# Query and key projections by seven block products, and some work at other places in the order

## The reference

```python
h = rmsnorm(x, norm_w)                    # (512, 1024)
proj = h @ w_in                           # split into:
#   dsa_qkv: 3 groups x (q, k, v) x 8 heads x 64;  dsa_z: 512
#   gdn_qkv: 3 x 512;  gdn_z: 512;  gdn_b, gdn_a: 8 each;  gate_a, gate_b: 1024 each
q, k = rope(q), rope(k)                   # t * cos + rotate_half(t) * sin, half = 32 of 64
o_a = dilated_mixture(q, k, v)            # windowed attention of 3 dilations, joined by softmax of their lse
y_a = (o_a * silu(dsa_z)) @ w_up_a
cqkv = silu(causal_depthwise_conv(gdn_qkv))
o_b = rmsnorm(gated_delta_rule(l2norm(q), l2norm(k), v, g(gdn_a), sigmoid(gdn_b)))
y_b = (o_b * silu(gdn_z)) @ w_up_b
x = x + (sigmoid(gate_a) * y_a + sigmoid(gate_b) * y_b) @ w_out
x = rmsnorm(x, final_norm_w)
```

## Time and profile before

| | us |
|---|---|
| median of 3 runs | 2187.51 |
| lowest, highest | 2183.54, 2192.11 |
| profiled execution | 2183.56 |
| its span | 2181.9 |
| mean granted PE clock | 0.964 |

### The profile page before, as it was taken

How to read it: one execution, slowest core, us unless ns; L and a number is a source line. 1 busy time by engine, 2 the same in 40 slices (tenths; PEclk the granted TensorE clock), 3 DMA queues, 4 the chain that set the end, 5 groups by cost and what they waited for, 6 DMA issues and landing times. The chain is left out here.

```text
span 2181.9 us, 31075 instructions
## 1 busy us (share of the span) xinstructions
PE 2028.5 (93%) x12920; PEld 1299.0 (60%) x12920; DVE 952.8 (44%) x1958; ACT 509.0 (23%) x1038; POOL 205.0 (9%) x202
## 2 busy tenths in 40 slices
PE   8999989989999899999998998897998999999987
PEld 3445767756567566685694464683885555544543
DVE  6672055633452425458414677738644221111102
ACT  1000163142122112353023255325222111100011
POOL 0001102302320233000000001301200000000001
PEclk9999999999899999999999999899799999999999
DMA  4222200110011773111122010000007999999996
GB/s 174 76 75 74 84 20 30 60 53 30 25 36 35 293 310 126 48 59 49 39 72 96 25 34 30 2 15 16 3 20 310 406 424 427 424 426 424 427 425 269
DMA packets 51692, 325.73 MB, mean 149 GB/s; under 512 B 6368, under 2 KB 9056, under 8 KB 33248
## 3 DMA queue, kind: packets, MB, share of 16 engines
q1 hardware_dynamic: 50256, 319.01, 36.9%
q0 software_dynamic: 1152, 4.19, 0.5%
q10 hardware_dynamic: 144, 0.52, 0.1%
HBM read 311.65 MB, written 9.96 MB: 147 GB/s over the span
## 5 line engine op out<-in xcount | busy, mean ns | idle before, releaser
L3700 PE MATMUL psum<-m_ring,m_xg 128*64 128x512 f32 x1024 | 226.2, 597 | 21.5 <-issue 20.4
L3700 PEld LDWEIGHTS psum<-m_ring,m_xg 128*64 128x64 f32 x1024 | 77.1, 138 | 167.3 <-issue 166.0
L419 PE MATMUL psum<-h,wring 128*128 128x512 f32 (+1 forms) x416 | 166.7, 549 | 10.8 <-PEq L93 5.6
L723 PE MATMUL psum<-x,wring 128*128 128x512 f32 x384 | 167.7, 599 | 6.8 <-DMA wring<-in_w1f 6.8
L723 PEld LDWEIGHTS psum<-x,wring 128*128 128x128 f32 x384 | 73.8, 193 | 99.7 <-issue 91.2
L3685 PEld LDWEIGHTS psum<-m_sel,m_htok 128*128 128x128 f32 x1024 | 118.3, 194 | 13.7 <-issue 12.2
L419 PEld LDWEIGHTS psum<-h,wring 128*128 128x128 f32 x416 | 78.4, 195 | 77.3 <-issue 65.5
L3685 PE MATMUL psum<-m_sel,m_htok 128*128 128x128 f32 x1024 | 122.6, 279 | 1.4 <-DVE m_sel L3676 1.4
L3710 DVE TENSOR_TENSOR m_hid<-rstd,psum 64x512 f32<-64x512 f32 x32 | 22.1, 691 | 232.1 <-ACT rstd L3706 221.7
L3725 PE MATMUL psum<-m_ring,m_hid_t 128*64 128x512 f32 x512 | 113.4, 595 | 1.0 <-issue 1.0
L3706 ACT ACTIVATE rstd<-psum 64x512 f32<-64x512 f32 x32 | 18.8, 588 | 324.7 <-PE psum L3700 313.4
(11 more groups left out here) (687 smaller groups left out, 3507.4 us busy)
## 6 DMA issues: line engine op xcount, KB each, us to landing
m_ring<-in_w_gate SPq DMA_DIRECT2D x32, 2048.0 KB, 26.9
m_ring<-in_w_up SPq DMA_DIRECT2D x32, 2048.0 KB, 28.3
m_ring<-in_w_down SPq DMA_DIRECT2D x64, 1024.0 KB, 24.6
wring<-in_w1f SPq DMA_DIRECT2D x60, 512.0 KB, 3.4
ada_ring<-in_w_ada SPq DMA_DIRECT2D x12, 2048.0 KB, 12.4
wring<-in_w2f SPq DMA_DIRECT2D x31, 512.0 KB, 3.4
expert_rows<-tmp SPq DMA_DIRECT2D x14, 512.0 KB, 28.9
wring<-in_w1v SPq DMA_DIRECT2D x12, 512.0 KB, 3.4
```

The source lines that it names most:

```text
L419: return nc.tensor.matmul(place(t, out), lhs, rhs, start=(k == 0), stop=(k == KD - 1))
L723: m = nc.tensor.matmul(K.psum[:, banks[t % 4]], ws.weights(first + t, k), h[:, k], start=(k == 0), stop=(k == KD - 1))
L3700: m = nc.tensor.matmul(K.psum[i * SLOTS:(i + 1) * SLOTS, UP + s], W.xg[:, k, s], w[:, k], start=(k == 0), stop=(k == KD - 1))
```

## The change

- `roped` uses `Pairs`: 12 pairs of which the first is plain. POOL makes the four differences of the weighted x (into v's not yet used part) and four folds per pair. ACT copies the parts into `raws` (gatedB, free at that time) and copies each whole tile once more with its 32-row quarters exchanged into `tmp` (four activations, `swap`). VectorE adds the parts, multiplies raw with cos into the output, `tmp` with sin, and adds. The sine table has its sign exchanged, as the rows are now exchanged first.
- `first_norm` gives the eight multiplications for h positions 0.12 to 0.47, so that they stand between the pairs.
- The SiLU of z moves from the end of `values` to `dilated_join`, behind its Exp; the join's last product waits for it (`zed`).
- `gdn_inputs` loses its sync program; its two loads are the first of `conv`'s sync program, under a global semaphore `ba_landed`. The two programs of the other side are laid out over 36 instead of 45.
- `out_project`: the first half of the next-to-last `total` goes ahead of the last part; ACT's squares get other positions.

```diff
@@ -548,6 +548,7 @@
...
         for k in range(KD):
+            yield 0.12 + 0.05 * k
             nc.vector.tensor_tensor(h[:, k], x[:, k], rate, ALU.mult).then_inc(K.normed, 1)
@@ -706,43 +707,77 @@
...
...
-def roped(nc, K, h, out, cos, sin, banks):
-
-    n, quarter, ws = 24, HD // 2, K.stream
-    first = ws.take(n)
+def roped(nc, K, h, out, cos, sin, diffs, folds, raws, banks):
+
+    n, quarter, ws = 12, HD // 2, K.stream
+    first = ws.take(2 * n)
+    two = Pairs(nc, K, lambda q: first + 2 * q, lambda q: (h, diffs), folds, banks, plain=1, ready=K.weighted)
+    raw = lambda q: lambda i: raws[:, 2 * (q % 2) + i]
+
+    def gpsimd(eng, sem):
+        yield 0.0
+        eng.wait_ge(K.weighted, KD)
+        two.halve(eng, nc.gpsimd, sem, h, diffs)
+        for q in range(n):
+            yield q / n
+            two.fold(eng, nc.gpsimd, sem, q)
...
     def tensor(eng, sem):
-        for t in range(n):
-            yield t / n
-            eng.wait_ge(*ws.arrived(first + t))
-            if t >= 4:
-                eng.wait_ge(sem["emptied"], t - 3)
-            for k in range(KD):
-                if t == 0:
-                    eng.wait_ge(K.weighted, k + 1)
-                m = nc.tensor.matmul(K.psum[:, banks[t % 4]], ws.weights(first + t, k), h[:, k], start=(k == 0), stop=(k == KD - 1))
-            m.then_inc(ws.used, 1)
+        for q in range(n):
+            for at in two.multiply(eng, sem, q, (1, 3, 2, 4)):
+                yield (q + at) / n
+
+    def scalar(eng, sem):
+        def swap(t):
+            two.whole(eng, sem, t // 2, t % 2)
+            if t >= 2:
+                eng.wait_ge(sem["roped"], t - 1)
+            of = raw(t // 2)(t % 2)
+            for p0 in range(0, P, quarter):
+                to = p0 ^ quarter
+                m = nc.scalar.activation(K.tmp[to:to + quarter, t % 2], of[p0:p0 + quarter], ACT.Copy)
+            m.then_inc(sem["swapped"], 1)
+
+        for q in range(n):
+            for i in range(4):
+                yield (q + (0.2, 0.36, 0.5, 1.05)[i]) / n
+                if q >= 2 and i < 2:
+                    eng.wait_ge(sem["roped"], 2 * (q - 2) + i + 1)
+                if q < two.plain and i == 2:
+                    swap(2 * q)
+                if q >= two.plain and i == 3:
+                    swap(2 * q)
+                two.copy(eng, sem, q, i, raw(q))
+                if q and i == 0:
+                    swap(2 * q - 1)
+        swap(2 * n - 1)
...
     def vector(eng, sem):
-        for t in range(n):
-            yield (t + 1.1) / n
+        def turn(t):
             if t == 0:
                 eng.wait_ge(K.tables, 2)
-            eng.wait_ge(ws.used, first + t + 1)
-            if t >= 2:
-                eng.wait_ge(sem["roped"], t - 1)
-            ps = K.psum[:, banks[t % 4]]
-            for p0 in range(0, P, quarter):
-                to, of = p0 ^ quarter, slice(p0, p0 + quarter)
-                nc.vector.tensor_tensor(K.tmp[to:to + quarter, t % 2], ps[of], sin[of], ALU.mult)
-            to, scaled, turned = out[:, t], K.tmp[:, t % 2], (ps, cos)
+            two.whole(eng, sem, t // 2, t % 2)
+            of, scaled, to, by = raw(t // 2)(t % 2), K.tmp[:, t % 2], out[:, t], cos
             if t >= 8:
-                to, scaled, turned = to.rearrange("p (a i) -> p a i", a=TT), strided(scaled), (strided(ps), strided(cos))
-            nc.vector.tensor_tensor(to, turned[0], turned[1], ALU.mult).then_inc(sem["emptied"], 1)
-            eng.wait_ge(sem["emptied"], t + 1)
+                of, scaled, to, by = strided(of), strided(scaled), to.rearrange("p (a i) -> p a i", a=TT), strided(cos)
+            nc.vector.tensor_tensor(to, of, by, ALU.mult).then_inc(sem["turned"], 1)
+            eng.wait_ge(sem["swapped"], t + 1)
+            nc.vector.tensor_tensor(K.tmp[:, t % 2], K.tmp[:, t % 2], sin, ALU.mult).then_inc(sem["turned"], 1)
+            eng.wait_ge(sem["turned"], 2 * t + 2)
             nc.vector.tensor_tensor(to, to, scaled, ALU.add).then_inc(sem["roped"], 1)
...
-    return Program(["emptied", "roped"], sync=ws.requests(first, n), tensor=tensor, vector=vector)
+        for q in range(n):
+            yield (q + 0.3) / n
+            if q:
+                turn(2 * q - 1)
+            for i in range(3):
+                yield (q + (0.6, 0.75, 0.9)[i]) / n
+                two.add(eng, sem, q, i, raw(q))
+            yield (q + 0.95) / n
+            turn(2 * q)
+        turn(2 * n - 1)
+
+    return Program(["swapped", "turned", "roped"] + two.SEMS, sync=ws.requests(first, 2 * n), gpsimd=gpsimd, tensor=tensor, scalar=scalar, vector=vector)
@@ -806,10 +841,6 @@
...
                 two.copy(eng, sem, q, i, raw(q))
-        for q in range(nz // 2):
-            for i in range(2):
-                two.whole(eng, sem, q, i)
-                nc.scalar.activation(z[:, 2 * q + i], z[:, 2 * q + i], ACT.Silu)
@@ -1153,6 +1184,8 @@
...
         nc.scalar.activation(low, low, ACT.Exp).then_inc(sem["exped"], 1)
+        for m in range(4):
+            nc.scalar.activation(z[:, m], z[:, m], ACT.Silu).then_inc(sem["zed"], 1)
@@ -1182,9 +1215,10 @@
...
             link(nc.vector.tensor_tensor(gated[:, m], gated[:, m], tmp, ALU.add))
+            eng.wait_ge(sem["zed"], m + 1)
             nc.vector.tensor_tensor(gated[:, m], gated[:, m], z[:, m], ALU.mult)
...
-    return Program(["ordered", "diffed", "exped", "weighed", "spread", "joined", "v"], tensor=tensor, scalar=scalar, vector=vector)
+    return Program(["zed", "ordered", "diffed", "exped", "weighed", "spread", "joined", "v"], tensor=tensor, scalar=scalar, vector=vector)
@@ -1214,7 +1248,7 @@
...
                                        [(K.halves, a["levelc"]), (K.gdn_gain[:], a["gdn_gain"]), (window, a["mask0"]), (causal, a["mask1"]), (order[:], a["order"])], 7),
-                  follow((168, roped(nc, K, x1, qk, cos, sin, range(4))), (113, values(nc, K, h, v, z, range(4, 8), diffs, folds))))
+                  follow((168, roped(nc, K, x1, qk, cos, sin, v[:].rearrange("p g u n -> p (g u n)")[:, 4 * CTX * KD // 2 // 2:].rearrange("p (i k n) -> p i k n", i=4, n=CTX), folds, gatedB, range(4))), (113, values(nc, K, h, v, z, range(4, 8), diffs, folds))))
         with ExitStack() as ph2:
@@ -1468,8 +1502,8 @@
...
     def vector(eng, sem):
-        def total(t):
-            for i in range(2):
+        def total(t, which=(0, 1)):
+            for i in which:
                 eng.wait_ge(sem["squared"], 2 * t + i + 1)
@@ -1508,13 +1542,15 @@
...
             more(q, 2)
+            if q == n - 1:
+                total(KD - 2, (0,))
             yield (q + 1.01) / n
             part(q, 3)
-        total(KD - 2)
+        total(KD - 2, (1,))
...
         for t in range(KD):
-            yield (t + 1.3) / KD
+            yield (t // 2 + (0.65 + 0.5 * (t % 2) if t < 2 else 0.93 + 0.13 * (t % 2))) / n
             two.whole(eng, sem, t // 2, t % 2)
@@ -2195,19 +2231,13 @@
...
...
-def gdn_inputs(nc, K, a, h, ba, beta, w_ba, bank, rep):
-
-    def sync(eng, sem):
-        yield 0.0
-        eng.dma_start(w_ba[:], a["w1ba"]).then_inc(sem["loaded"], 16)
-        eng.dma_start(rep[:], a["rep"]).then_inc(sem["rep"], 16)
-        eng.wait_ge(sem["rep"], 16)
+def gdn_inputs(nc, K, h, ba, beta, w_ba, bank):
...
             if t == 0:
-                eng.wait_ge(sem["loaded"], 16)
+                eng.wait_ge(K.ba_landed, 32)
             for k in range(KD):
@@ -2218,7 +2248,7 @@
...
...
-    return Program(["loaded", "rep", "done"], sync=sync, tensor=tensor, scalar=scalar)
+    return Program(["done"], tensor=tensor, scalar=scalar)
@@ -2243,7 +2273,7 @@
...
         x_c, folds = sb("g_xc", [P, 4, S + 3], p2), sb("g_folds", [P, 4, KD // 2 * P], p2)
-        weave(nc, "gp", conv(nc, K, h, diffs, folds, x_c, qkv, range(4)), in_turn((27, join), (12, gdn_inputs(nc, K, a, h, ba, beta, w_ba, 4, seeds.rep)), over=45))
+        weave(nc, "gp", conv(nc, K, h, diffs, folds, x_c, qkv, range(4), [(w_ba[:], a["w1ba"]), (seeds.rep[:], a["rep"])]), in_turn((27, join), (12, gdn_inputs(nc, K, h, ba, beta, w_ba, 4)), over=36))
     held.close()
@@ -2274,7 +2304,7 @@
...
...
-def conv(nc, K, h, diffs, folds, x_c, qkv, banks):
+def conv(nc, K, h, diffs, folds, x_c, qkv, banks, loads):
@@ -2326,7 +2356,15 @@
...
...
-    return Program(["convd", "v"] + two.SEMS, sync=ws.requests(first, 2 * n), gpsimd=gpsimd, tensor=tensor, scalar=scalar, vector=vector)
+    def sync(eng, sem):
+        yield 0.0
+        for to, of in loads:
+            eng.dma_start(to, of).then_inc(K.ba_landed, 16)
+        for at in ws.requests(first, 2 * n)(eng, sem):
+            yield at
+        eng.wait_ge(K.ba_landed, 16 * len(loads))
+
+    return Program(["convd", "v"] + two.SEMS, sync=sync, gpsimd=gpsimd, tensor=tensor, scalar=scalar, vector=vector)
@@ -4088,8 +4126,8 @@
...
                       24 + len(values) + 4 + 12 + 4 + len(merges[0]) + len(merges[1]) + len(outs))
```

(6 more changed lines are left out.)

## The result

The changed kernel takes 2160.86 us (median of 4 runs, 2160.04 to 2164.92), the kernel before in the same comparison 2185.53 (2178.57 to 2192.11): ratio 0.9892, interval 0.9872 to 0.9912, or 24.7 us. Forecast were 2160.9 and 26.6 us. The profiled execution took 2161.64, its span 2159.9.

The account below looks back on a forecast made before the run. PE, busy 93% of the span, was taken as the bound. 17.5 - 1.5 - 1.6 + 3.5 + 2.0 + 5.5 + 0.5 + 0.7 = 26.6 us off the median 2187.51 gave 2160.9 us; range 2153 to 2168, with rivals and run spread 2149 to 2174.

Parts of the forecast that it names:

- Seven products, 17.5 less 1.5 less 1.6: Query and key projections: less PE work saves 17.5 us, minus 1.5 for VectorE-POOL collisions and 1.6 waiting at pair 1.
- charge of 1.5 for collisions: Projections: 0.3 us lost in each of six pairs with both strides and h, rounded to 1.5 us (0 to 12).
- the start of pair 1: Projections: PE waits for POOL's first folds after the plain pair, costing 1.6 us (0.5 to 5).
- rival B: Projections: VectorE and POOL obstruct each other and set the pace, about 1 us more in ten pairs; 2171 us, chance 0.12.
- it just holds: Projections, strided pairs with h: VectorE is free at 8.9 us, its adds end near 10, PE needs them at 10.4.
- rival C: Projections: ACT's swap copies, a us each, pace PE; at a = 1.2, 34 us lost, 2195 us; chance 0.04.
- It decides from about a = 1.1: Projections: the time per ACT swap copy, a in us, from which late copies were said to decide; 0.61 was expected.
- h between the pairs, 0: Projections: h is needed only 120 us later, so moving its normalisation costs 0, apart from 0.69 us VectorE work per pair.
- SiLU, 3.5 and 2.0: End of first stage: moving z's SiLU saves 3.5 us of PE wait, and 2.0 (0 to 3) of low clock in dilated attention.
- Beta loads and layout, 5.5 and 0.5: Convolution stage: early beta weights save 5.5 us of wait and low clock; the join over 36 saves 0.5 (-1 to 1.5).
- Output sums, 0.7: End of output projection: last squares start about 0.6 us earlier and context norm is not blocked; 0.7 us saved (0 to 1.5).
- squares no longer block the context norm: Output projection: reordered squares stop holding up the context norm, counted within the 0.7 us saving.

Follow-up runs that it names:

- second trace: The changed kernel run once more, unchanged, in five rounds against the kernel before (also traced again): 2159.32 us (6 runs), ratio 0.9884.
- first experiment: The kernel before with only the seven-product projections, the exchanged sine sign and h normalised between the pairs: 2166.7 us, ratio 0.992.
- the kernel with the earlier differences: The changed kernel with the four differences of weighted x made by VectorE, not POOL, and beta groups later: 2155.72 us; 2153.72 when repeated.

## Why the prediction was right, step by step

- **Seven products, 17.5 less 1.5 less 1.6.** The pace was as read from the earlier trace rows: 12.09 us per pair, forecast 12.1. The charge of 1.5 for collisions was not needed, no pair from 2 to 11 waits; the start of pair 1 cost 2.32 instead of 1.6. The first and fourth fold ended at 26.30 and 31.33, hardly later than in the sum (near 26 and 31), but PE came to them at 25.18 and not at 25.8. In the second trace it cost 1.54, of which 0.98 were a wait for VectorE's adds; the prediction looked for no such wait at pair 1. In sum 15.8 and 14.6 us (two traces, each against its own before), forecast 14.4.
- **Collisions, rival B.** The estimate that it just holds was right. In the changed kernel's pair from 98.83 VectorE is busy for 9.46 of 12.09 us, where its operations alone are 7.7. With the product for h it is free 8.7 us after the pair's start (in the sum 8.9), the first two adds end at 9.4, and PE needs them at 10.4. Two added operations per tile turned it into B and worse. Collisions go the way of the rule of the Trainium skill ("SBUF — State Buffer", "Who interferes with whom"): a VectorE product with two SBUF inputs that took 0.69 us alone took 2.84 us beside a POOL difference of 2.78, and it ended 0.55 us after that difference. These are the rows of the changed kernel:

```profile
21.85 2.78 POOL L226 TENSOR_TENSOR v<-x,v 128x1024 f32<-128x1024 f32 x1
22.34 2.84 DVE L548 TENSOR_TENSOR rstd<-rstd,gatedA 128x512 f32<-128x512 f32 x1
```

- **Swap copies, rival C.** 0.628 us for 32x512, forecast 0.61; with a = 0.91 its sum gave 0.8 us per pair where 0.67 of wait and 0.93 of pair length were seen. "It decides from about a = 1.1" hides that by the same sum copy 2 is late from a = 0.81 on.
- **h between the pairs, 0.** "Cost 0" is true of the changed kernel, so the sum is right. What the prediction missed is what the move is worth: it did not ask what the old place would have cost beside the new work. It is 9.8 us, more than half of the projections' gain. The fault was to price the move in the old schedule, where VectorE's late start hurt nobody, and not in the new one, where the adds of pair 1 free PE's banks.
- **SiLU, 3.5 and 2.0.** 3.34, and 2.1 or 0.7 (by the trace of before that one takes). The wait was there in every trace, the clock's fall varies.
- **Beta loads and layout, 5.5 and 0.5.** 4.74 and 3.08: this is the term that was most oversized. The wait goes from 2.08 to 0.33, and one of two waits for VectorE's adds goes (0.92 and 0.94 before, 0.93 after). From the start of the wait to the third group of products behind the first beta group PE took 10.72 and 10.83 us before and takes 7.36 and 7.54 now: 3.3 us, not 5.5. The term's 3.4 us of clock was priced as if it went with the wait, and it doesn't always. The first experiment, with the whole wait but no fall, took 7.37. In two traces with the changed order (the experiments with the SiLU and with the output sums back) the clock did not fall there, and the stage took 104.9; so it did with the later beta groups. The second trace's 1.8 us more come from the stage's start: there 64 small matmuls run at the low clock in both traces, without a wait that the change touches, and for longer in the second (the first trace's row, then the second's):

```profile
330.71 7.63 PE L1167 MATMUL psum<-d_stat,order 32*128 32x8 f32 x64
...
331.35 9.15 PE L1167 MATMUL psum<-d_stat,order 32*128 32x8 f32 x64
```

- **Output sums, 0.7.** 2.97. Undersized: I did not follow the context squares in ACT's queue, though "squares no longer block the context norm" was the right mechanism.
- The hit to a tenth of a us is luck. The forecast started from 2187.51 for the kernel before, which is 2185.53 beside the changed one, and its gain was 1.9 us too large against the timed one; the two errors cancel. Against the stage lengths the first-block terms were 1.3 us (two traces' mean) too small, with the projections and the output sums too small and the beta term too large. Single runs of the kernel before differ by up to 15.7 us among the fifteen beside the second set of experiments (2175.52 and 2191.26).

## What to carry to other kernels

A change of algorithm for a bound engine pays as its new pace says, if each helper's due time is worked out within one period. The helper with the least slack then decides what every other VectorE instruction costs, and moves that were free before (h's products) become part of the price. ACT's and VectorE's queues are read in order: look for the instruction that waits in front of the one that the bound engine needs. A gain in an early stage is to be read from that stage's length in the trace, since the granted clock in later stages moves the whole by as much as a small change does (here by 2.2 us in the gated delta stage, and 10 us over the second block, whose differences were not followed up).

## What the runs showed of the hardware

- Beside POOL's folds eight VectorE operations of 0.61 us (4.90 in all) took 12.40, while their POOL partners went from 1.27 to 1.6 to 1.8 us: VectorE lost more than POOL. A fold and a VectorE operation together took 1.67 us (the fourth fold of the changed kernel starts at 29.62, the next at 31.29), less than 0.61 and 1.22 us one after the other, the distances to the next start where neither is held up (the second from the kernel with the earlier differences, 21.58 to 22.80): nearly a full block of the other engine, but not quite. Adds with one input in PSUM kept 0.42 (median) throughout.
- The clock falls in the same place in some runs only: behind waits of 2.06 to 2.16 us for the beta weights it fell in both traces of the kernel before and not in the first experiment, with the same work of PE before it. With the loads moved and a wait of 0.33 to 0.51 us it fell in five of seven traces, both of the changed kernel among them. At the first scores it fell in all four traces with a wait of 4.2 us and in one of nine with 0.87. What decides is open.
- Activations of 32x128 start 0.23 us apart when issued back to back, though each lasts 0.29.
